# Attention's output projection as three rounded products, its second weight half rounded and split by GpSimd

## What is computed

```python
def swa_sink_attention(hn, w_q, sinks, w_o, k_band, v_band, bias):
    q = (hn @ w_q).reshape(bsz, n, CHUNK, B_KV_HEADS, B_GROUP, B_HEAD_DIM) * (B_HEAD_DIM ** -0.5)
    s = jnp.einsum('bnqhgd,bnkhd->bnhgqk', q, k_band).astype(jnp.float32) + bias
    ...
    p = jnp.exp(s - m)
    p = p / (jnp.sum(p, axis=-1, keepdims=True) + jnp.exp(sink - m))
    o = jnp.einsum('bnhgqk,bnkhd->bnqhgd', p.astype(v_band.dtype), v_band)
    return o.reshape(bsz, L, B_Q_HEADS * B_HEAD_DIM) @ w_o
```

## Time and profile before

| | |
|---|---|
| median of 3 runs | 1414.27 us (1411.99 to 1415.44) |
| the profiled execution, its own time | 1412.82 us |
| its span (first to last instruction) | 1411.0 us |
| busy: PE, DVE, ACT, POOL | 1377.2, 500.5, 278.2, 89.2 us |
| mean granted PE clock | 0.991 of full speed |
| first record of scores(0) / of the experts' first matmul | 443.60 / 527.28 us |
| the chain that ended last: PE in all, the experts' gate and up matmuls (L2172) | 90%, 41% |

### The profile page before, as it was taken

One profiled execution on the slowest core, in us unless ns is written; L12 is line 12 of the kernel. 1 busy time (PEld: TensorE's weight loads), 2 busy tenths in 40 slices (PEclk: granted clock), 3 DMA queues, 4 the chain that ended last, 5 costly groups with the idle time before them and its releaser, 6 DMA issues.

```text
span 1411.0 us, 31798 instructions
## 1 busy us (share of the span) xinstructions
PE 1377.2 (98%) x14487; PEld 759.2 (54%) x14487; DVE 500.5 (35%) x1030; ACT 278.2 (20%) x522; POOL 89.2 (6%) x75
## 2 busy tenths in 40 slices
PE   6999999999999989999999999999999999999997
PEld 6998967999989653333333333333333333333333
DVE  5767355554545345233042042042041141240222
ACT  5640234434455410000000000000000000000002
POOL 4340010000000000000100100100100100100000
PEclk8999999999999999999999999999999999999999
DMA  7542016555553359999999999999999999999991
GB/s 276 180 143 98 4 60 217 194 178 183 173 209 120 157 222 413 405 426 412 393 425 415 399 422 415 396 421 421 401 418 413 411 407 420 410 408 421 407 421 54
DMA packets 92987, 436.32 MB, mean 309 GB/s; under 512 B 5816, under 2 KB 29552, under 8 KB 84544
## 3 DMA queue, kind: packets, MB, share of 16 engines
q1 hardware_dynamic: 87232, 423.64, 75.1%
q0 software_dynamic: 3616, 7.42, 2.2%
q10 hardware_dynamic: 2016, 3.38, 0.7%
HBM read 427.46 MB, written 6.96 MB: 308 GB/s over the span
## 4 chain that ended last, share of the span: by engine, by line
PE 90%; DVE 4%; ACT 3%; issue 1%; DMA 1%; POOL 1%; POOLq 0%; DVEq 0%; ACTq 0%
PE bank L2172 41%; PE bank L2198 13%; PE bank L2201 6%; PE bank L1645 5%; PE bank L1646 5%; PE bank L1647 5%; PE bank L2065 2%; PE bank L1871 2%; PE bank L1681 1%; DVE ws L1057 1%; PE bank L2222 1%; ACT qkv_hi L680 1%; PE bank L1786 1%; PE bank L1769 1%; PE bank L2051 1%
## 5 line engine op out<-in xcount | busy, mean ns | idle before, releaser
L2172 PE MATMUL bank<-ring,xt 128*32 128x448 f32 x6144 | 580.3, 539 | 0.4 <-DVE xt L1546 0.4
L2172 PEld LDWEIGHTS bank<-ring,xt 128*32 128x32 f32 x6144 | 199.7, 110 | 372.4 <-issue 369.5
L1496 DVE TENSOR_TENSOR ws<-ws,bank 64x448 f32<-64x448 f32 x96 | 82.3, 988 | 526.4 <-ACT ws L952 526.4
L2198 PE MATMUL bank<-ring,hidden_turned 128*32 128x512 f32 x1680 | 218.8, 593 | 0.0
L952 ACT ACTIVATE ws<-bank 64x448 f32<-64x448 f32 x96 | 51.9, 540 | 653.5 <-PE bank L2172 653.5
L2201 PE MATMUL bank<-ring,hidden_turned 128*32 128x256 f32 x1680 | 129.2, 379 | 0.0
L2201 PEld LDWEIGHTS bank<-ring,hidden_turned 128*32 128x32 f32 x1680 | 54.6, 110 | 125.6 <-issue 125.6
L1645 PE MATMUL bank<-x_hi,weights_hi 128*128 128x256 f32 x320 | 90.3, 282 | 1.3 <-issue 1.3
L1646 PE MATMUL bank<-x_lo,weights_hi 128*128 128x256 f32 x320 | 90.3, 282 | 0.0
L1647 PE MATMUL bank<-x_hi,weights_lo 128*128 128x256 f32 x320 | 89.4, 279 | 0.0
L1244 DVE TENSOR_TENSOR weights_lo<-weights,weights_hi 128x1024 fp32r<-128x1024 f32 x62 | 73.1, 1221 | 40.4 <-ACT weights_hi L801 40.4
(11 more groups left out here) (340 smaller groups left out, 1399.1 us busy)
## 6 DMA issues: line engine op xcount, KB each, us to landing
ring<-in_moe_w_gate SPq DMA_DIRECT2D x64, 1792.0 KB, 13.4
ring<-in_moe_w_up SPq DMA_DIRECT2D x64, 1792.0 KB, 15.7
ring<-in_moe_w_down SPq DMA_DIRECT2D x64, 1792.0 KB, 14.7
weights<-in_a_w_in SPq DMA_DIRECT2D x7, 2048.0 KB, 9.0
weights<-in_ffn_w_up SPq DMA_DIRECT2D x11, 1024.0 KB, 5.3
weights<-in_ffn_w_gate SPq DMA_DIRECT2D x11, 1024.0 KB, 5.2
weights<-in_ffn_w_down SPq DMA_DIRECT2D x11, 1024.0 KB, 4.9
weights<-in_a_w_out SPq DMA_DIRECT2D x2, 2048.0 KB, 8.0
```

The costliest lines, as they stand in the source:

```text
L1496: dve.tensor_tensor(to, by_row[0], by_row[1], ALU.mult).then_inc(m_hid, 1)
L2172: m = pe.matmul(by_run(bank[2 * b + c][LANE * g:LANE * g + LANE, 0:2 * PART]), xe[:, kt, LANE * b:LANE * b + LANE], w_[:, c, g % 2], start ...
L2198: pe.matmul(bank[6][LANE * g:LANE * g + LANE, :], hT[h][g // 2][:, r], moving(D * j + 512 * (g % 2), 512), start=begin, stop=end, skip_gro ...
```

## The change

The projection becomes `product`s: 32 x 3 = 96 float32r matmuls of 128x512 in place of 32 float32 ones. Its operands have to be split:

- Weight half 0: ACT rounds it in four pieces of 128x1024 (`out_weights`) between `queries(1)` and `exps(0)`; POOL subtracts each piece in place.
- Weight half 1: POOL does both, a copy into the high part and the subtraction, four times, once `s_qmm` is 4 (the high part lies where the last queries' weights were).
- The heads' output: ACT rounds bank 5 into `oTh` (`heads_round(g)`), behind `exps(g + 1)` and, for group 0, behind `queries(3)`; DVE then subtracts into `oTl` in place of its copy to `oT`, at the same place in its list.
- The parts lie where three early ring buffers were, so the ring's addresses are dealt out anew: buffer 0 waits for `s_qmm` 4, buffer 1 for `s_pt` 16 (the last transposes), 2 and 3 for `s_aw` 3, 4 to 7 for `s_aw` 4.

```diff
+        oTh, oTl = rounded("attn_out_hi", KT * T, ws0 + 4 * 16384), rounded("attn_out_lo", KT * T, ws0 + 4 * 6144)
+        woh, wol = (whi[0], wlo[0]), (qlo[0], qlo[1])
...
+        RING_FREE = ((s_qmm, 4), (s_pt, 16), (s_aw, 3), (s_aw, 3), (s_aw, 4), (s_aw, 4), (s_aw, 4), (s_aw, 4))
...
-                    e_load(k, r2[k], e_in(w, 0, 0, pair), *((s_qmm, 4) if k < 3 else (s_aw, 3) if k == 3 else (s_aw, 4)))
+                    e_load(k, r2[k], e_in(w, 0, 0, pair), *RING_FREE[k])
...
             for k in (1, 2, 4):
+                if k == 4:
+                    for piece in range(8):
+                        c = slice(1024 * (piece % 4), 1024 * (piece % 4) + 1024)
+                        if piece < 4:
+                            pool.wait_ge(q_hi, 16 + piece + 1)
+                        else:
+                            if piece == 4:
+                                pool.wait_ge(loaded[1], 16 * (PRE_A[1] + 2))
+                                pool.wait_ge(s_qmm, 4)
+                            link(pool.tensor_copy(woh[1][:, c], slot[1][:, c]))
+                        pool.tensor_tensor(wol[piece // 4][:, c], slot[piece // 4][:, c], woh[piece // 4][:, c].bitcast(F32),
+                                           ALU.subtract).then_inc(q_lop, 1)
                 norm_rstd(k)
...
+            def out_weights(j):
+                c = slice(1024 * j, 1024 * j + 1024)
+                if j == 0:
+                    act.wait_ge(loaded[0], 16 * (PRE_A[0] + 2))
+                    act.wait_ge(s_qmm, 2)
+                act.activation(woh[0][:, c], slot[0][:, c], ACT.Copy).then_inc(q_hi, 1)
+
+            def heads_round(g):
+                act.wait_ge(s_pv, g + 1)
+                act.activation(view(oTh, 0, KT, T)[:, 2 * g:2 * g + 2, :], view(bank[5], 0, 2, T), ACT.Copy).then_inc(s_x0h, 1)
+
             queries(0)
             queries(1)
+            for j in range(4):
+                out_weights(j)
             exps(0)
...
                 if g == 0:
                     queries(3)
+                heads_round(g)
...
             def heads_out(g):
-                dve.wait_ge(s_pv, g + 1)
-                dve.tensor_copy(oT[:, 2 * g:2 * g + 2, :], view(bank[5], 0, 2, T)).then_inc(s_oT2, 1)
+                dve.wait_ge(s_x0h, 4 + g + 1)
+                v = lambda x: view(x, 0, KT, T)[:, 2 * g:2 * g + 2, :]
+                dve.tensor_tensor(v(oTl), view(bank[5], 0, 2, T), v(oTh).bitcast(F32), ALU.subtract).then_inc(s_oT2, 1)
...
                     for kt in kts:
-                        m = pe.matmul(bank[2 * t + q][:, :], oT[:, kt, t * P:(t + 1) * P], g8[q][:, kt, :],
-                                      start=first and kt == kts[0], stop=last and kt == kts[-1],
-                                      skip_group_check=True)
+                        if t == 0 and kt % 2 == 0:
+                            pe.wait_ge(q_lop, 6 + 4 * q + kt // 2 + 1)
+                        m = product(bank[2 * t + q][:, :], xh_[:, kt, :], xl_[:, kt, :], wh[:, kt, :], wl[:, kt, :],
+                                    first and kt == kts[0], last and kt == kts[-1])
```

More of the change, by code:

```diff
@@ L172, in trunk @@
         ring = [nc.alloc_sbuf_tensor_at(f"ring{k}", [P, 2 * HALF], F32, offset=at)
-                for k, at in enumerate((ws0 + 4 * 20480, ws0 + 4 * 24064, slot0 + 4 * 2 * KT * 512, slot0,
-                                        slot0 + 4 * KT * 512, ws0 + 4 * 12288, ws0 + 4 * 15872, ws0 + 4 * 8704))]
+                for k, at in enumerate((slot0 + 4 * 2 * KT * 512, ws0 + 4 * 8704, slot0, ws0 + 4 * 20480,
+                                        slot0 + 4 * KT * 512, ws0 + 4 * 24064, ws0 + 4 * 12288, ws0 + 4 * 15872))]
         hT = [[nc.alloc_sbuf_tensor_at(f"hidden_turned{k}{b}", [P, HALF // 4], F32, offset=at) for b, at in enumerate(ats)]
@@ L266, in trunk @@
         sc = [view(ws, 9216 + 2048 * k, 2 * NC, T) for k in range(2)]
-        oT = view(ws, 16384, KT, T)
         pT = [view(ws, 13312 + 512 * k, 4, P) for k in range(2)]
@@ L378, in trunk @@
         m_rows, m_added, m_turn, m_free = (sem(n) for n in ("m_rows", "m_added", "m_turn", "m_free"))
-        ring_in0, ring_in1, ring_in5, ring_in6, ring_in7 = (
-            sem(n) for n in ("ring_in0", "ring_in1", "ring_in5", "ring_in6", "ring_in7"))
-        ring_in = [ring_in0, ring_in1, loaded[2], loaded[0], loaded[1], ring_in5, ring_in6, ring_in7]
+        ring_in1, ring_in3, ring_in5, ring_in6, ring_in7 = (
+            sem(n) for n in ("ring_in1", "ring_in3", "ring_in5", "ring_in6", "ring_in7"))
+        ring_in = [loaded[2], ring_in1, loaded[0], ring_in3, loaded[1], ring_in5, ring_in6, ring_in7]
         m_gh, m_gu, m_d = (sem(n) for n in ("m_gh", "m_gu", "m_d"))
@@ L389, in trunk @@
         PRE_A = [n + NF for n in PRE]
-        RING_PRE = [0, 0, PRE_A[2] + 1, PRE_A[0] + 2, PRE_A[1] + 2, 0, 0, 0]
+        RING_PRE = [PRE_A[2] + 1, 0, PRE_A[0] + 2, 0, PRE_A[1] + 2, 0, 0, 0]
+        RING_FREE = ((s_qmm, 4), (s_pt, 16), (s_aw, 3), (s_aw, 3), (s_aw, 4), (s_aw, 4), (s_aw, 4), (s_aw, 4))
         w_in, conv_w = ins["a_w_in"], ins["a_conv_w"]
@@ L2061, in merge @@
                 for q in halves:
-                    if first:
-                        pe.wait_ge(loaded[q], 16 * (PRE_A[q] + 2))
+                    xh_, xl_ = (view(x, 0, KT, T)[:, :, t * P:(t + 1) * P] for x in (oTh, oTl))
+                    wh, wl = view(woh[q], 0, KT, 512), view(wol[q], 0, KT, 512)
                     for kt in kts:
-                        m = pe.matmul(bank[2 * t + q][:, :], oT[:, kt, t * P:(t + 1) * P], g8[q][:, kt, :],
-                                      start=first and kt == kts[0], stop=last and kt == kts[-1],
-                                      skip_group_check=True)
+                        if t == 0 and kt % 2 == 0:
+                            pe.wait_ge(q_lop, 6 + 4 * q + kt // 2 + 1)
+                        m = product(bank[2 * t + q][:, :], xh_[:, kt, :], xl_[:, kt, :], wh[:, kt, :], wl[:, kt, :],
+                                    first and kt == kts[0], last and kt == kts[-1])
                     if last:
```

## The result

The changed kernel takes 1419.3 us, the median of 8 runs (1416.75 to 1421.81); the kernel before takes 1413.38 beside it. The ratio is 1.0045, 95% interval 1.0035 to 1.0054: slower by 5.9 us, within the range, with the forecast 4.7 us too high. The profiled execution took 1417.25, 4.4 more than before's; its span is 1415.4. In this kernel lines are shifted: L1372 and L1373 are now L1400 and L1401, L1379 is L1407, L1384 is L1412, L2020 is L2049, L2034 is L2063, L2051 is L2080.

What follows compares the result with a forecast made beforehand. PE was taken to bound the kernel. `values(2)` 14.0 us late, less 6.2 saved, gives 7.8; with 2.2 of clock +10.0, so 1422.8 profiled and, 1.5 above, a median of 1424 us; range 1415.5 to 1430.

Steps and rivals of the forecast that it cites:

- PE's saving: In the projection, 32 float32 matmuls (28.0 us) become 96 rounded ones (21.8 us): 6.2 us saved, all on the path.
- POOL's lock on DVE: DVE operations reading two SBUF tensors stand still until POOL's running operation ends; worked through with the order, `values(2)` 14.0 us late.
- The rival without contention: POOL's work does not hold up DVE's divisions; only the order's 2.5 us stay: -3.7 us, 1410.6 to 1414; chance 15%.
- The rival in which the four divisions pass together: Group 1's four divisions follow each other without POOL between: `values(2)` 10.3 late, +4.1 to +6.3, 1418.4 to 1420.6; chance 20%.
- The other three wait for one POOL operation each: In group 1, the divisions after the first each wait for a POOL operation, done at 474.1, 475.7 and 478.5.
- The order term: `heads_round(1)` behind `exps(2)` on ACT delays DVE's low part and group 2's division: PE starts `values(2)` 2.5 us late.
- The clock: PE, with about 7 us of work from 468 to 488, loses granted clock: 2.2 us, of 0 to 3.4.
- no wait for `q_lop`: POOL's pieces are all in time for the projection at 492.5, so `q_lop` costs nothing.
- the ring: Buffers 1 and 2 load later than before, at no cost; if their cover were gone, one load, 4.3 us.

Runs made afterwards that it cites:

- before_pool: The kernel before plus eight POOL operations of 128x1024 (copy, subtraction, four times, in free space) behind `s_qmm` 4: 1419.91 us, ratio 1.0045.
- plain_mm: The changed kernel with 32 float32 matmuls of the high parts in place of the 96, low parts left out of the product: 1422.70 us, ratio 1.0073.
- all_dve: The change without POOL: ACT rounds all eight weight pieces, DVE subtracts them and makes both parts of the heads' output: 1408.06 us, ratio 0.9967 to the kernel before.
- before_order: The kernel before, with ACT copying bank 5 into `oT` where the change rounds it and DVE's own copy waiting for that: 1418.32 us, ratio 1.0035.
- heads_dve: The changed kernel with DVE making both parts of the heads' output, none on ACT, POOL's work as changed: 1420.76 us, ratio 1.0051.
- after_fill: The changed kernel with idle matmuls in PE's waits of groups 1 and 2 (18, 10 and 30): 1417.27 us, ratio 1.0031.
- before_order_fill: The kernel before with ACT's copy of bank 5 ahead of DVE's, plus 18 idle matmuls ahead of `values(2)`: 1414.88 us, ratio 1.0010.

## Why the prediction was right, and where its sizes were off

**The direction and the mechanism held.** The experts' stage is unchanged, PE's saving is on the path, and two terms outweigh it: the order and POOL's lock on DVE. The rival without contention is ruled out by before_pool. The rival in which the four divisions pass together is too: two of them were held up.

**Group by group.** `values(0)` was forecast 1.9 late and came 1.6 late; `values(1)` stood at 470.06 for 471.5 and stretched over 8.4 us for 9.3; POOL's last subtraction ended at 479.92 for 482.1.

**The lock.** The rows show a DVE operation on two tensors of SBUF ending with POOL's. L1400, a single-input operation, is caught as well: 0.67 and 0.89 us for 0.17, the second ending at 477.50 with POOL's cast. That such an operation can contend is what the Trainium skill says in "SBUF — State Buffer", section "Who interferes with whom". The prediction had it held in group 2 from 480.9 to 482.1; it was held 0.7. What it is worth by itself no run shows.

**The step that failed in size: "The other three wait for one POOL operation each".** Forecast for the four divisions were 471.4, 474.1, 475.7 and 478.5; they ended at 470.0, 470.3, 473.0 and 474.3. The second got through in the gap between POOL's cast and the subtraction that waits for it, 468.83 + 1.03 to 469.94, where the working gave every such gap to POOL. One subtraction's worth of waiting fell away with it; a cast of 1.04 in place of 1.2 and a start at 465.4 in place of 466.1 did the rest. Group 1 is done at 474.3 instead of 478.5, and `values(2)` is 9.6 late, not 14.0. That is 4.4 of the 5.6 us by which the profiled executions' difference, 4.4, fell short of the forecast 10.0. The clock (0.6 for 2.2, below) and the earlier `scores(0)` (0.65) make 2.3 more; PE's smaller saving takes 1.0 back. The median lies 2.05 over the profiled execution, for 1.5 in the forecast.

**PE's saving: 6.2 forecast, 5.2 measured.** The term was sized too large twice: the first two products stand 0.34 apart, and with that 36 take 8.43 us up to `values(3)` (487.56 to 495.99), 0.234 each for 0.227; the 12 float32 matmuls before took 10.41 (478.58 to 488.99), 0.868 each for 0.875. 32 x (0.868 - 3 x 0.234) is 5.3. With `values(2)`, PE needs 12.96 us for 14.95 up to `values(3)`: 2.0 for three eighths of the work. Over the whole projection the traces of the changed kernel and of plain_mm agree on 5.2. all_dve, with nothing else in the way, gained 4.6.

**The order term: 2.5 forecast, 2.0 measured** (before_order). What the prediction did not draw out is that the two terms meet. Because `heads_out(0)` waits for ACT behind `queries(3)`, group 1's division moves from 460.7, ahead of POOL's work, to 467.0, into the middle of it. POOL alone makes `values(2)` 2.2 late, the order alone 2.0, both together 9.6 in the changed kernel, 1.6 of which was there at `values(0)`. Without the order term, in heads_dve, `values(2)` is 3.5 late (476.79, with `scores(0)` at 442.88). So beside POOL's work the order is worth 6.2 us at `values(2)`, not 2.5. The prediction's working had the meeting in its times for group 1, but named 2.5 as the order's price.

**The clock: 2.2 forecast, in the wrong place.** It expected a fall that runs partly behind 488. The fall from 474 to 482 came and cost nothing, since PE had to wait until 483.03 in either case (after_fill). "TensorE: Matmul & The Clock Gate" of the Trainium skill, part 1, has TensorE's clock throttled by default and released by activity. The traces agree: 0.50 behind the waits of before_order (478 to 486), 1.00 in the same place with idle matmuls in the wait (before_order_fill). What the clock did cost came in places that no step named: most likely the 2.4 in the median through group 0, and the 0.6 behind the second router in the profiled execution, where the loss was 5.1 us of clock for 3.4 before, part of it in waits (read from the windows, not tested in the changed kernel). The median's 5.9 is the 4.4 of the profiled executions, plus the 2.05 by which the changed kernel's median lies over its own (group 0), less the 0.56 by which before's does.

**What held at nothing**: no wait for `q_lop`, none for the ring; the four divisions of group 0 took 1.56 as before, their POOL pieces being over.

## What to carry to other kernels

Work on an idle engine is not free if the engine on the critical chain stands still beside it: here POOL's operations, each off the path, put 5 us into DVE's division of group 1 (7.2 busy for 1.9). The same subtractions took half the time in DVE's own gaps and cost nothing. And a rounding on ACT that DVE has to wait for belongs ahead of the long work in ACT's list; if it stands behind, price not only its delay but what the delayed work then runs into.

A wait of 2.5 us ahead of dense TensorE work cost 5.7 in before_order, since the clock came down on what stood behind it; ask of every new wait what runs right behind it. Where PE waits again anyway, the fall is free.

## What the runs showed of the hardware

- The price of a clock fall depends on where it lands: nothing in the changed kernel from 474 to 482, 3.3 us in before_pool, 3.4 in before_order (3.1 and 4.1 if each run is taken against the kernel before of its own group).
- Idle matmuls in the wait held the clock. 18 of 128x256 ahead of `values(2)` gave back 3.4 us, 11 ahead of `values(0)` took 2.4 off a median.
- Behind a wait of 1.57 us the clock fell to 0.50 in the trace of after_fill; behind 1.58 us in the same place of the changed kernel's trace it stayed at 1.00. Executions of after_fill differ by 2.3 us (1417.23 and 1419.58), most likely by this.
- POOL's cast of 128x1024 takes 1.04 us and its subtraction 2.35; DVE's subtraction of the same shape takes 1.22. In the 0.1 us between POOL's cast and the subtraction that depends on it, two waiting DVE divisions got in (to 470.3). The masked scores, which read a bank and one tensor, took 0.27 to 0.41 us beside POOL's subtraction at 474.20 as they did at 455.88, with POOL idle.
- The reciprocal of 128x8 took its 0.20 us beside POOL's cast (468.94), while the single-input L1400 was held to the end of one (476.61).
